# A two-layer fp32 block on one core: weight splits and norm scalings moved within ScalarE's and VectorE's queues

## What is computed

```python
def memory_attention(h, mem_n, w_q, w_kv, w_out):      # 4 heads
    sc = jnp.einsum('bshd,bmhd->bhsm', q, k).astype(jnp.float32) * XA_HEAD_DIM ** -0.5
    p = jax.nn.softmax(sc, axis=-1).astype(v.dtype)
    return jnp.einsum('bhsm,bmhd->bshd', p, v).reshape(b, s, D_MODEL) @ w_out
...
    yg = y.reshape(b, s, G, SSD_D_INNER // G)          # the scan's norm, 8 groups
    yg = yg * lax.rsqrt(jnp.mean(yg * yg, axis=-1, keepdims=True) + LN_EPS)
    y = (yg.reshape(b, s, SSD_D_INNER) * norm_g.astype(jnp.float32)).astype(x.dtype)
    return y @ out_proj
...
        h = layer_norm(DN_ALPHA * h + mix, ln_mix_g[i], ln_mix_b[i])
        ff = conv_ffn(h, ffn_up[i], ffn_conv_w[i], ffn_conv_b[i], ffn_down[i])
        h = layer_norm(DN_ALPHA * h + ff, ln_ffn_g[i], ln_ffn_b[i])
```

## Time and profile before

| | |
|---|---|
| median of 3 runs | 1296.28 us (1294.85 to 1296.31) |
| the profiled execution | 1293.25 us, of which span 1291.5 us |
| TensorE busy | 1257.9 us, 97% |
| VectorE busy | 927.8 us, 72% |
| ScalarE busy | 680.5 us, 53% |
| GpSimd busy | 82.3 us, 6% |
| clock granted to TensorE | 0.999 of full speed |

### The profile page before, as it was taken

One profiled execution on the slowest core, in us unless ns is written; L12 is line 12 of the kernel. 1 busy time (PEld: TensorE's weight loads), 2 busy tenths in 40 slices (PEclk: granted clock), 3 DMA queues, 4 the chain that ended last, 5 costly groups with the idle time before them and its releaser, 6 DMA issues. The chain is left out here.

```text
span 1291.5 us, 18650 instructions
## 1 busy us (share of the span) xinstructions
PE 1257.9 (97%) x7688; PEld 1114.4 (86%) x7688; DVE 927.8 (72%) x1288; ACT 680.5 (53%) x867; POOL 82.3 (6%) x94
## 2 busy tenths in 40 slices
PE   7999999999999999999999998999999998999997
PEld 7878999989988888889998887888888977888886
DVE  5565857874447655575987987788878766788877
ACT  4555354443544444445777664566654563566652
POOL 2010000100000000000003331000000000000000
PEclk9999999999999999999999999999999999999999
DMA  8664646665535556645556554655554633655651
GB/s 282 207 183 130 187 140 182 212 187 204 164 107 168 189 191 192 196 150 181 173 179 224 194 180 147 196 195 194 185 182 133 199 118 99 200 190 195 196 188 41
DMA packets 159748, 227.98 MB, mean 177 GB/s; under 512 B 5517, under 2 KB 122001, under 8 KB 159536
## 3 DMA queue, kind: packets, MB, share of 16 engines
q1 hardware_dynamic: 156544, 216.68, 52.3%
q0 software_dynamic: 2816, 9.52, 2.2%
q10 hardware_dynamic: 304, 0.59, 0.1%
HBM read 225.68 MB, written 1.10 MB: 176 GB/s over the span
## 5 line engine op out<-in xcount | busy, mean ns | idle before, releaser
L1241 DVE TENSOR_TENSOR wlo<-raw,whi 128x2048 fp32r<-128x2048 f32 (+3 forms) x188 | 419.6, 2244 | 118.9 <-ACT whi L789 118.3
L789 ACT ACTIVATE whi<-raw 128x2048 fp32r<-128x2048 f32 (+2 forms) x187 | 347.7, 1873 | 17.3 <-DMA raw<-in_w_xkv 6.6
L2038 PE MATMUL psum<-h_both,whi 128*128 128x512 f32 x714 | 254.7, 396 | 0.0
L2006 PE MATMUL psum<-h_both,whi 128*128 128x256 f32 x704 | 200.6, 285 | 0.7 <-DVE wlo L1241 0.7
L2037 PE MATMUL psum<-h_both,wlo 128*128 128x256 f32 x714 | 199.3, 279 | 0.3 <-DVE h_both L1286 0.3
L2008 PE MATMUL psum<-h_both,wlo 128*128 128x256 f32 x704 | 199.1, 283 | 0.0
L2007 PE MATMUL psum<-h_both,whi 128*128 128x256 f32 x704 | 199.1, 283 | 0.0
L2006 PE MATMUL psum<-whi,r_hi 128*128 128x512 f32 (+1 forms) x464 | 180.9, 390 | 1.4 <-DVE arena L1583 0.7
L2008 PE MATMUL psum<-whi,r_lo 128*128 128x512 f32 (+1 forms) x464 | 178.1, 384 | 0.0
L2007 PE MATMUL psum<-wlo,r_hi 128*128 128x512 f32 (+1 forms) x464 | 178.0, 384 | 0.0
L2038 PEld LDWEIGHTS psum<-h_both,whi 128*128 128x128 f32 x714 | 134.0, 188 | 27.6
(11 more groups left out here) (327 smaller groups left out, 1860.5 us busy)
## 6 DMA issues: line engine op xcount, KB each, us to landing
raw<-in_ffn_up SPq DMA_DIRECT2D x44, 1024.0 KB, 5.1
raw<-in_w_in SPq DMA_DIRECT2D x32, 1024.0 KB, 5.6
raw<-in_ssd_in_proj SPq DMA_DIRECT2D x24, 1024.0 KB, 5.4
raw<-in_ffn_down SPq DMA_DIRECT2D x22, 1024.0 KB, 4.8
raw<-in_w_up SPq DMA_DIRECT2D x16, 1024.0 KB, 5.5
raw<-in_w_down SPq DMA_DIRECT2D x16, 1024.0 KB, 4.9
raw<-in_w_xkv SPq DMA_DIRECT2D x8, 1024.0 KB, 5.3
raw<-in_ssd_out_proj SPq DMA_DIRECT2D x8, 1024.0 KB, 5.1
```

The lines of the kernel that those rows point to most:

```text
L789: A(whi[u % SLOTS][:, 0:kt * n], raw[u % SLOTS][:, 0:kt * n], ACT.Copy).then_inc(hi_split, 1)
L1241: V.tensor_tensor(wlo[s][:, 0:kt * n], raw[s][:, 0:kt * n], whi[s][:, 0:kt * n].bitcast(F32), ALU.subtract).then_inc(lo_split, 1)
L2006: M(o, a_hi, b_hi, start=start, stop=False)
L2038: return M(b[:, :], w_hi_k, h_both[:, :, k, :], start=False, stop=k == kt - 1)
```

## The change

No instruction is added or removed. ScalarE's and VectorE's queues get another order in four places; TensorE's, GpSimd's and SyncE's are as they were.

```diff
@@ ssd_steps
-    steps.append(("tail", SSD_HEADS))
+    steps += [("tail", SSD_HEADS), ("none", 0), ("none", 0), ("scale", 3)]
@@ scalar, memory attention: the loop over k, then
-            for _ in range(4):
-                hi()
+                if k >= XA_HEADS:
+                    hi()
+            hi()
@@ scalar, scan
-                    if what == "tail":
-                        group_norm(3)
+                    if what == "scale":
+                        group_norm(h)
@@ scalar, latent attention
             for k in range(7, MLA_HEADS + 3):
                 attend(k)
-            hi()
-            hi()
+                if k in (8, 9):
+                    hi()
@@ vector, layer_norm
-                def finish(t):
+                def finish(t, beside=None):
...
                     tile_inverse(t, RMS_EPS if rms else LN_EPS, rms)
+                    if beside is not None:
+                        beside()
...
                 if lo_name is not None:
-                    tile_lo(0)
+                    tile_lo(0, 0)
                 add(1, 1)
-                finish(1)
+                finish(1, (lambda: tile_lo(0, 1)) if lo_name is not None else None)
                 if lo_name is not None:
-                    tile_lo(1)
+                    tile_lo(1, 0)
+                    tile_lo(1, 1)
@@ vector, memory attention: the loop over k, then
-            for _ in range(3):
-                lo()
+                if k >= XA_HEADS:
+                    lo()
@@ vector, latent attention
             attend(5)
+            attend(6)
             lo()
-            attend(6)
             attend(7)
             lo()
             attend(8)
             attend(9)
             lo()
+            lo()
             attend(10)
             lo()
             ffn_pads()
-            lo()
             layer_norm(lambda c, t: ("ao", c, t), 5, lo_name="h7")
```

More of the change, by code:

```diff
@@ L1400, in finish, with tile_lo @@
                             .then_inc(normed, 1)
[L1402 to L1407, removed]
+                def tile_lo(t, c):
+                    key, k = (lo_name, t, c), slice(4 * c, 4 * c + 4)
+                    b = wait_bank(dve, key)
+                    part(h_lo[:, k, P * t:P * t + P], b[:, :].rearrange("p (k t) -> p k t", k=4), h_hi[:, k, P * t:P * t + P])\
+                        .then_inc(done(key), 1)
                 for slot in (1,) if rms else (0, 1):
```

## The result

The changed kernel takes **1285.62 us** in the median (1285.02 to 1286.66, 4 runs), the kernel before 1295.57 on the same chip (1294.07 to 1296.31, 4 runs): ratio 0.9929, 95% interval 0.9917 to 0.9942. That is 9 to 10 us faster, where 1289.0 was forecast, with 1286.9 as the fast end of the range. The direction was right and the time is outside the range.

A forecast was written before the change was run, and what follows sets the result against it. TensorE, busy 1257.9 of 1291.5 us, bounds the kernel, so order can win only its waits. Terms 0.8 + 0.9 + 2.9 + 1.2 + 1.2 = 7.0, plus 0.3, off the median 1296.28 gave 1289.0 us, range 1286.9 to 1292.6.

The forecast's parts named there:

- Memory attention, 0.8: Behind the memory attention's last head: splits made two heads earlier end TensorE's stall near 385 us, 0.8 us.
- End of the scan, 0.9: Scan's end: half splits moved into idle time bring the low parts and h5's first add earlier, 0.9 us.
- The wait of 2.61: TensorE's longest wait, ended by h5's norm at 804.75 us; sign: it should shrink to 1.7 to 2.1.
- Tile 1 of the norms, 2.9: Norms of h5, h6, h7: low part put behind `ms` ends TensorE's waits at tile 1; 1.0, 0.9 and 1.0 us.
- Latent attention, both parts, 2.4: Latent attention: weight splits reordered shorten the "mo" 1 wait by 1.2 us and the end with h7's tile 0 by 1.2.
- the surest sign: New TensorE idle of about 0.3 us before `last_two`'s third step, showing the weight transfer is in the chain.
- Sum, 7.3: Whole kernel: terms of 7.0 us plus 0.3 for gaps between starts; profiled span falls from 1291.5 to 1284.2 us.
- the one from the execution to the median: Whole kernel: profiled execution lies 3.0 us below the shown runs' median 1296.28, so forecast off the median is 1289.0.
- Rival 1: Scan's end: GpSimd's power shut out by VectorE's queued half splits, two halves later; 1291.2 us, chance 0.08.
- Rival 2: Norms' tile 1: the wait moves to tile 0's products or the gain instead of ending; 1291.9 us, chance 0.09.
- Rivals 3 and 4: Latent attention's end: slow weight transfer; 7.1 us landing gives 1290.8, chance 0.06; 16 us gives 1299.7, chance 0.02.
- Rival 5: FFN or MLP: gains given back because a transfer or VectorE sets the pace; about 1293.5 us, chance 0.06.

The follow-up runs named there:

- f2: The changed kernel with the scan's two edits undone: 1286.85 us in the median of 5 runs, 1286.57 without one run of 7094.76.
- e1: The kernel before with the latent attention's edits alone: 1291.03 us, ratio 0.9973.
- e2: The kernel before with the layer norms' edits alone: 1293.09 us, ratio 0.9988.
- e3: The kernel before with the memory attention's edits alone: 1294.14 us, ratio 0.9998.
- f3: The changed kernel with the latent attention's edits undone on ScalarE and VectorE: 1290.81 us.
- h1: The kernel before, nothing moved, with TensorE doing useless identity transposes in its six waits of 0.9 us or more from h5's norm on: 1293.32 us, ratio 0.9989.
- f4: The changed kernel with VectorE's weight split in front of h5's first add moved behind the scaling of tile 0: 1285.80 us.
- g2: The changed kernel with one more half of a weight split moved into idle time at the scan's end on ScalarE and VectorE: 1284.59 us, ratio 0.9918.
- h2: The changed kernel without its latent attention edits, with its three remaining waits filled by useless transposes on TensorE: 1288.60 us, ratio 0.9953.

## Why the prediction was wrong, by its steps

- **Memory attention, 0.8.** Right: 1.0.
- **End of the scan, 0.9.** Right: 0.84 in the trace, 0.8 to 1.1 by f2. The wait of 2.61 is 2.16, just outside the 1.7 to 2.1 that was to be seen.
- **Tile 1 of the norms, 2.9.** Right: 1.1 in h5, 1.0 in h6, and no wait left in h7. The power took 0.54 to 0.56 beside the low part, as rows 6 had it, and the gain took 1.28 us as before, so it didn't wait for the power's last 0.1.
- **Latent attention, both parts, 2.4, with 1.0 for tile 1 of h7: 3.4.** The trace has 3.75. What came on top of the forecast is mainly at the end: the 0.3 for the wait in the third step of `last_two` wasn't there: TensorE's trace has no gap at it, with a landing of 5.1 us instead of 5.3. The prediction had called that idle time the surest sign, and it was missing.
- **Sum, 7.3, and the span, 1284.2.** The trace has 8.0 and a span of 1284.1, with a start that was 0.6 late. That the span fits to 0.1 is luck, since the late start hides most of what the terms lack. The steps on waits held; their terms are small by 0.7 together.
- **The step that failed is the one from the execution to the median:** "It lies 3.0 below the median of the runs shown [...] Off the median the forecast is 1289.0." I carried those 3.0 us over as if they belonged to every execution of both kernels. They don't, and they are two things. Some 1.6 us were the draw of three runs: with the 1294.68 us of the 33 runs the same sum gives 1287.4, inside the range, still 1.8 above what was measured. The other 1.4 are how far the kernel before's median lies above this execution. It had no fall of the clock before its last product, and the median's clock, 0.997, is that of one fall more: 3.4 us of it and the 3.3 us at the end, at half the clock, make 0.9974 of 1291.5 us (an estimate from the windows of e1 and before). Falls came at h5 (e1, e2, e3, f3) and at "mo" 1 (e2, f3), behind waits that this change shortens or ends. Filling the waits takes 1.5 us off the median of before (h1). The changed kernel's median, 1285.62, is at the level of its profiled execution, 1285.89, which had no such fall. So what the change wins in the median is 8.0 for the waits and about 1.5 for the falls, 9.5; measured were 9.95, with the high draw in it, and 8.7. Worked out from the execution, 1293.25 - 7.3, the forecast would have been 1286.0. The table of before already spoke for it: its clock was 0.999, and the three timed runs all lay 1.6 us or more above it.
- **A rival that was missing:** that the clock differs between executions and depends on these very waits. It belonged into the range, whose fast end was set by the terms alone.
- **A reading that was wrong:** that VectorE released every wait of 0.7 us or more. In front of h6's first product behind tile 1's transposes TensorE stood idle for 0.86 us with no releaser shown, and has 0.97 after. The change doesn't touch it, and the sum doesn't use it.
- **Rival 1** fell: the scan's power took 1.93 us as before, with three splits in a row beside it. **Rival 2** fell but for what the sum had priced: in h6 the low part now ends at 995.30 and a product that needs it starts at 995.35, which costs about 0.2 us. **Rivals 3 and 4** fell: 5.1 us of landing. **Rival 5** fell: 8.0 us arrived at the end.

What stays open: why f3 had a lower clock in all five runs, and f2, with the longer wait in front of h5, no fall in its profiled one. e2 is like f3 in this: both have the norms' edit without the attention's, and not one of their 16 runs has more than 0.997. So an edit may also bring falls. Against 6 of 33 in the kernel before that can still be chance, and no run here was made for it. Where a fall may come in relation to a wait wasn't tried. That every fall in before's runs is behind one of the six filled waits is shown only by h1's clocks, since only profiled executions say where.

## What to carry to other kernels

When the profiled execution lies outside the timed runs, find out what it has not before adding a difference to their median; here its granted clock (0.999) was half of the answer, and three runs being too few for a median the other half. Compare kernels at the same mean clock. A wait of TensorE can cost more than it lasts: the falls of the clock behind a few waits cost about 1.5 us of the median here. And when a wait moves without shrinking (f4), look for the engine that is busy without a gap behind it: take work out of its stretch into idle time ahead (g2), don't reorder it.

## What the runs showed of the hardware

The granted clock fell to 1.2 GHz for 3.4 us, beginning 0.4 to 2.5 us behind the end of waits of 2.6, 2.14 and 1.33 us, in some executions and not in others with the same waits. A fall cost 1.2 to 1.6 us in the traces, and 1.1 us by f3 and h2 (2.2 for two). With the waits filled by transposes without any use, which depend on nothing, no run of h1 or h2 (16) had a clock under 0.998, and the kernel before was 1.5 us faster.

GpSimd's power, queued while VectorE had three half splits in a row, each with two SBUF inputs, took 1.93 us, no more than beside a single one before: it waited for one of them and not for three. The Trainium skill, SBUF — State Buffer, "Who interferes with whom", states the exclusion and not who goes next when one instruction waits and more are queued; here it was GpSimd.
